# Starting the moba attention one quarter of a unit later in a two-block transformer kernel

## What is computed

```
q_b = apply_rope(rms_norm(q_b, g_q_moba), cos, sin)     # 256 x 4 x 128
k_b = apply_rope(rms_norm(k_b, g_k_moba), cos, sin)
s   = (q_b . k_b) * 128**-0.5, masked to k <= t
o_b = softmax(s) @ v_b
merged = sigmoid(gate_a) * (o_a @ w_br_dsa) + sigmoid(gate_b) * (o_b @ w_br_moba)
x = x + gt_m * (merged @ w_out)
```

## Time and profile before

| | before |
|---|---|
| time, median of 3 runs | 1490.16 us (1490.03 to 1490.28) |
| the profiled execution, its own time | 1494.77 us |
| span from its first to its last instruction | 1492.7 us |
| PE busy | 1450.2 us, 97% |
| DVE busy | 849.1 us, 57% |
| ACT busy | 689.3 us, 46% |
| mean granted TensorE clock | 0.990 |

### The profile page before, as it was taken

The page is one execution under the profiler, slowest core; times in us unless marked ns, Lnnn a source line. Parts: engine busy times, 40 slices in busy tenths (PEclk is TensorE's granted clock), DMA queues, the critical chain, the costliest instruction groups (busy, mean ns, idle before and its releaser), DMA issues.

```text
span 1492.7 us, 17981 instructions
## 1 busy us (share of the span) xinstructions
PE 1450.2 (97%) x6910; PEld 1161.4 (78%) x6910; DVE 849.1 (57%) x1033; ACT 689.3 (46%) x880; POOL 36.1 (2%) x53
## 2 busy tenths in 40 slices
PE   6999999999999999999999999999999998999998
PEld 3757777788888888888888888788888865788887
DVE  2687766554556545466755455565445658655444
ACT  2454454444344444454454444754444667554442
POOL 0010100000000000000000000200000020000000
PEclk9999999999999999999999999999999989999999
DMA  9763767455564655546555655555555510455551
GB/s 343 272 224 113 244 222 264 133 196 187 179 196 156 211 179 187 194 157 200 182 177 189 188 179 196 148 191 178 195 184 183 191 41 29 141 178 189 190 190 70
DMA packets 188163, 271.13 MB, mean 182 GB/s; under 512 B 8380, under 2 KB 134148, under 8 KB 188100
## 3 DMA queue, kind: packets, MB, share of 16 engines
q1 hardware_dynamic: 186448, 267.01, 54.3%
q10 hardware_dynamic: 1492, 2.98, 0.7%
q0 software_dynamic: 160, 0.26, 0.2%
HBM read 269.19 MB, written 1.05 MB: 181 GB/s over the span
## 4 chain that ended last, share of the span: by engine, by line
PE 84%; DVE 6%; ACT 3%; DMA 3%; issue 2%; SPq 1%; POOL 0%; ACTq 0%; DVEq 0%
PE bank L1821 25%; PE bank L1823 25%; PE bank L1822 25%; DVE w_lo_ring L1327 2%; PE bank L1851 2%; DMA raw_ring<-in_w_mod_dram 1%; ACT w_hi_ring L982 1%; PE bank L1991 1%; DMA raw_ring<-in_w_in_dram 1%; PE bank L2123 1%; PE bank L2045 1%; PE bank L2144 1%; SPq L885 1%; PE bank L1879 0%; PE bank L1959 0%
## 5 line engine op out<-in xcount | busy, mean ns | idle before, releaser
L1327 DVE TENSOR_TENSOR w_lo_ring<-raw_ring,w_hi_ring 128x2048 fp32r<-128x2048 f32 (+1 forms) x226 | 513.8, 2277 | 401.6 <-ACT w_hi_ring L1270 329.8
L1821 PE MATMUL bank<-w_hi_ring,h_hi 128*128 128x512 f32 x1360 | 543.5, 400 | 2.2 <-DVE h_lo L1475 1.0
L1823 PE MATMUL bank<-w_hi_ring,h_lo 128*128 128x512 f32 x1360 | 531.8, 391 | 0.0
L1822 PE MATMUL bank<-w_lo_ring,h_hi 128*128 128x512 f32 x1360 | 530.9, 390 | 0.0
L1270 ACT ACTIVATE w_hi_ring<-raw_ring 128x2048 fp32r<-128x2048 f32 x158 | 302.8, 1917 | 295.8 <-PE bank L1823 292.5
L1821 PEld LDWEIGHTS bank<-w_hi_ring,h_hi 128*128 128x128 f32 x1360 | 256.2, 188 | 66.5 <-issue 15.6
L1823 PEld LDWEIGHTS bank<-w_hi_ring,h_lo 128*128 128x128 f32 x1360 | 255.8, 188 | 54.9
L1822 PEld LDWEIGHTS bank<-w_lo_ring,h_hi 128*128 128x128 f32 x1360 | 256.4, 189 | 49.4
L1821 PE MATMUL bank<-w_hi_ring,f_hi 128*128 128x512 f32 (+1 forms) x456 | 177.1, 388 | 0.0
L1823 PE MATMUL bank<-w_hi_ring,f_lo 128*128 128x512 f32 (+1 forms) x456 | 176.0, 386 | 0.0
L1822 PE MATMUL bank<-w_lo_ring,f_hi 128*128 128x512 f32 (+1 forms) x456 | 175.7, 385 | 0.0
(11 more groups left out here) (259 smaller groups left out, 873.1 us busy)
## 6 DMA issues: line engine op xcount, KB each, us to landing
raw_ring<-in_ffn_w_gate_up_dram SPq DMA_DIRECT2D x176, 512.0 KB
raw_ring<-in_ffn_w_down_dram SPq DMA_DIRECT2D x44, 1024.0 KB
raw_ring<-in_w_in_dram SPq DMA_DIRECT2D x22, 1024.0 KB
raw_ring<-in_w_gate_up_dram SPq DMA_DIRECT2D x44, 512.0 KB
arena<-in_w_mod_dram SPq DMA_DIRECT2D x18, 1024.0 KB, 7.1
raw_ring<-in_w_down_dram SPq DMA_DIRECT2D x11, 1024.0 KB
raw_ring<-in_conv_w_in_dram SPq DMA_DIRECT2D x16, 512.0 KB
raw_ring<-in_w_mod_dram SPq DMA_DIRECT2D x6, 1024.0 KB
```

What stands on the lines that cost most here:

```text
L1327: dve.tensor_tensor(w_lo[:, u % RING, 0:words], raw[:, r % RING, 0:words], w_hi[:, u % RING, 0:words].bitcast(F32), ALU.subtract).then_inc ...
L1821: pe.matmul(dst, hi, whi, start=start, stop=False)
L1822: pe.matmul(dst, hi, wlo, start=False, stop=False)
L1823: return pe.matmul(dst, lo, whi, start=False, stop=stop)
```

## The change

The transposes of kb's keys move from behind quarter 0 to behind quarter 1. `spread` gets an argument that leaves quarters empty ahead of the steps, and the ten steps are spread over the 15 that are left. By its integer division they stand behind quarters 2, 3, 5, 6, 8, 9, 11, 12, 14 and 15. So steps 0, 2 and 4 move one quarter back and the other seven stay. Step 4 moves from the end of the second part to the first quarter of the third, which in the list puts it behind the gate chunk's copy, the top-k piece and the split of unit 13. No instruction is added, removed or altered, and no load is moved in the list.

```diff
-    def spread(steps, parts):
-
-        n = 4 * parts
-        quarters = [sum(steps[k * len(steps) // n:(k + 1) * len(steps) // n], []) for k in range(n)]
+    def spread(steps, parts, behind=0):
+
+        n = 4 * parts - behind
+        quarters = [[]] * behind + [sum(steps[k * len(steps) // n:(k + 1) * len(steps) // n], []) for k in range(n)]
         return [quarters[4 * p_:4 * p_ + 4] for p_ in range(parts)]
...
-    inside = spread(steps, 4)
-    part("ga", 0, 0, 2, [topk(0, 0)], [tgroup("kb", 2) + inside[0][0]] + inside[0][1:])
+    inside = spread(steps, 4, 1)
+    part("ga", 0, 0, 2, [topk(0, 0)], [[], tgroup("kb", 2) + inside[0][1]] + inside[0][2:])
```

## The result

The changed kernel takes 1493.24 us, the median of 20 runs, against 1490.41 us for the kernel before in 20 runs beside it: +2.83 us, ratio 1.002 with a 95% interval of 1.0012 to 1.0029 (+1.8 to +4.3 us). One of the 20 runs, 1818.32 us at a mean granted clock of 0.751, was in a slower state and is left out of the ratio, which like all ratios here is estimated from the runs and need not be the quotient of the two medians. The forecast was +1.42 us. So the change costs something, about twice what was forecast, and just about the 0.2% that the prediction took as the limit of what can be told.

A forecast was written before the change was run, and what follows sets the result against it. PE was taken as the bound, busy 97% of the span. The terms -1.41 (first stall), 0 (second) and +2.83 (new stall) gave +1.42 us, 1490.16 to 1491.58 us, with a range of 1488.6 to 1493.6.

The forecast's parts named there:

- Part 1: First ga-chunk stall, at kb's transposes: moved one quarter later they meet their release, and step 1 comes 1.41 us earlier.
- Part 2: Second ga-chunk stall, at step 3's transposes: stays 1.58 us; moving step 2 costs nothing, PE stays 1.41 us ahead.
- Part 3: Step 5's transposes: new stall of 2.83 us, as step 4 stands behind unit 13's split; PE passes 1.42 us late.
- Part 4: From step 6 through the rest of the kernel: the whole 1.42 us loss goes on, nothing takes it up.
- The clock: Behind the new stall at step 5's transposes: granted clock assumed to stay 1.00, leaving the sum at +1.42 us.
- the rival: Clock falls behind the new stall, in quarters 10 and 11: 1.72 us on top, +3.14, so 1493.30; chance 0.18.
- the late stretch: Late in the kernel, PE busy 2.40 of 4 us, then clock 0.70 and 0.87: 1.72 us lost; called thin throughout.
- the clock is under 1.00 there: Sign of being wrong: granted clock below 1.00 in the ga chunk, around the new stall.
- the win did not stay: Rival at step 4 in the ga chunk: DVE in time, no third stall, -1.41 us, so 1488.75; chance 0.08.
- the loss is not absorbed: Rival behind the ga chunk: a later wait not following PE absorbs the loss, 1490.2; chance 0.06.
- Low stretches elsewhere: Rival in later work: a low clock stretch comes or goes, 1.72 us either way, 1493.30 or 1489.86; chance 0.05 each.
- The call of no change beyond 0.2%: Whole kernel: time judged the same within about 0.2% (3.0 us, 1487.2 to 1493.1), chance 0.78.

The follow-up runs named there:

- the two kernels that part the edit: Changed kernel with step 4 back behind quarter 7: 1489.62 against 1489.98 us; kernel before with step 4 alone moved behind quarter 8: 1494.30 against 1489.98 us.
- the repeat: The changed kernel, unaltered, profiled and timed again with 12 runs against the kernel before: 1491.68 against 1489.58 us, ratio 1.0017.
- the second single execution: The changed kernel, unaltered, profiled in one more execution without timed runs: 1496.06 us.
- the filled stall: Changed kernel with unread constant products on PE ahead of step 5's transposes: 12 products 1493.85 against 1489.98 us, 6 products 1491.74 against 1490.03 us.

## Why the prediction was right, and where it was off

Counted from the start of L1974 in either trace, its steps came out so:

- **Part 1.** Kb's transposes start 3.88 us behind L1974 in both kernels, in the changed one without a wait. Step 1's score product comes 1.34 us earlier (forecast 1.41). Right.
- **Part 2.** The second stall is 1.56 us (forecast 1.58). Right.
- **Part 3.** The remainder of unit 13 starts 2.37 us earlier (forecast 2.41), step 5's transposes stall for 2.85 (2.83) and pass 1.46 late (1.42). Right, and the two kernels that part the edit give -1.37 for the gain and +2.86 for the loss: their sum, 1.49, is what the changed kernel shows with the clock at 1.00, 35.62 - 34.11 = +1.51.
- **Part 4.** The loss goes on to the end of the chunk, which is 3.09 later in the first profile: the 1.46, with the fall of the clock on top. At the second mark 2.89 of it are left, and 1.57 in the execution where the clock held (239.89 - 107.96 = 131.93 against 130.36). So hardly any of it is absorbed there.
- **The clock.** This is the step that was off: "I take the clock to hold". It fell in three of the four profiled executions of the changed kernel. From step 5's transposes to step 6's score product takes 133.91 - 128.98 = 4.93 us there, against 3.33 in the execution where it held (131.73 to 135.06): 1.60 us, where the rival had priced 1.72 from a stretch late in the kernel. Of the rival only the chance, 0.18, was too small. That the clock would hold had been argued from the dense work on both sides, and from the first stall of before, which is little more than half as long. That row could not bear it: in the chunk the clock held through all stalls of up to 1.6 us, in all seven profiles that have none longer (before, and the kernels with a remainder, with kb or with step 4 put elsewhere), and fell behind most of 2.85.

Nor was the late stretch thin throughout: in the earlier trace rows PE is busy 3.67 and 4.00 of 4 us where the clock reads 0.70 and 0.87. And the trace of before itself has a fall with dense work on both sides, which the prediction left out. Projection matmuls run without a gap until 233.9 and again from 239.25 on. Between them stand small groups of matmuls with waits of 0.38 and 0.97 us, and behind these the clock is low from about 239.7 to 243.0 us (timeline of PE in before, where the second wait is in the row at 238.34 shown above; then a window of half a microsecond of it):

```profile
236.29 1.07 PE L1991 MATMUL bank<-const,arena 128*128 128x128 f32 x8 [0.38 <-DVE arena L1540]
```

```profile
240.00:240.50 0.50, 0.50 (x3) 0.40 (x2) 0.50 (x1) 0.00 (x0) 0.00 (x0) 0.50 1.04 401
```

All fourteen profiles (before, four of the changed kernel, nine of other edits) have these two waits, and in six the clock falls behind them. So dense work on both sides was no reason to take the clock to hold, and the length of one stall alone doesn't decide it.

One of the prediction's own signs of being wrong, "the clock is under 1.00 there", came. Of the other rivals, the win did not stay (the stall is there) and the loss is not absorbed. Low stretches elsewhere do come and go between executions of the changed kernel, and the granted clock of the runs of before varies too (0.990 to 0.997 in one set); the time alone can't part them from the change.

Three in four of +3.09 and one in four of +1.51 make +2.70, near the measured +2.83, whose interval leaves the forecast's own +1.42 out; four executions are few for such a mean, and the repeat gave +2.10. The call of no change beyond 0.2% and the range, 1488.6 to 1493.6, held, but the upper end was reached by a rival, not by the forecast's case. That the call held is in part luck: the prediction counted a fallen clock as slower, and the clock fell in most executions, but not in all.

The Trainium skill, page "TensorE: Matmul & The Clock Gate", section "Why this matters for your kernels", warns against idle gaps between bursts in mid-kernel. Most executions of the changed kernel agree (0.50 behind 2.85 us of stall); the second single execution and the kernel with step 4 moved alone, with the same stall and 1.00, show that a gap of this length need not count.

What stays open: why the clock falls in one execution and not in another of the same program. That the stall is its cause rests on place and on counts (low in the chunk in three of the five profiles with this stall and an idle PE, each time beginning 0.3 to 1.0 us after PE went on, and in none of the nine others), and the filled stall agrees, but with two filled executions that could be chance.

## What to carry to other kernels

Where an engine takes a static list in order, moving a small urgent item past a long piece of work can cost whoever waits that piece and what the piece itself waits for (here 2.85 us, behind a remainder of 2.29 us that waits for ACT's copy). The cheaper edit is the reverse, to put the long piece, if nobody needs it soon, behind the small ones: three such moves took 2.55 us off the chunk. Price a new stall with and without the clock's fall, and look for every fall that the trace of the kernel before already has, not only for one that resembles the change. And when the time of a whole run varies by more than the effect, compare the length between two fixed instructions of the trace: the chunk repeated within 0.03 us over the three executions in which the clock fell, while 35 runs of before on one chip spread from 1485.2 to 1496.1.

## What the runs showed of the hardware that was not expected

- The clock behind one and the same stall of 2.85 us falls to 1.2 GHz in some executions and stays at 2.4 GHz in others. Where it falls, it does so 0.3 to 1.0 us after PE has begun again and stays low for about 3.4 us (130.0 to 133.4 in the first profile), which makes the chunk 1.57 to 1.60 us longer.
- The clock also falls near 239 us, behind waits of at most 0.97 to 0.98 us with dense projection matmuls after them, in six of fourteen profiles.
- Low stretches elsewhere come and go between executions of the same kernel, in the changed one at 35 to 45, 235 to 245, 1215 to 1230 and 1260 to 1270 us. Its span was 1487.0 us in an execution that has none between 135 and 1485 us, and 1493.0 in one that has two there.
- A plain f32 product of 128x256 stands in the trace as two matmuls of 0.22 us each (24 in 5.34 us for 12 products).
